# Three RMS norms of a two-block network: per-token roots applied at other places, and the slabs behind them in token halves

## The reference

```python
x = x + mix @ w_out                                   # end of the mixers of block one
h2 = rmsnorm(x, ln2)
x = x + jnp.square(jax.nn.relu(h2 @ w_mlp1)) @ w_mlp2
h3 = rmsnorm(x, ln3)
x = x + jax.nn.sigmoid(h3 @ w_pg) * (p @ w_pp)        # embedding gate
x = rmsnorm(x, ln_f)
# block two, even layer
h = rmsnorm_2(x, pre_g)
u = h @ w_in_ab
qa, ka, va, oa, za, ia, fa, qb, kb, vb, zb = split_cols(u, EVEN_SPLITS)
qk = silu(causal_dwconv(concat([qa, ka]), conv_w))    # 4 taps over the tokens
ig = ia + b_i
lf = log_sigmoid(fa + b_f)
ha = mlstm(q, k, va, ig, lf)
```

## Time and profile before

| | us |
|---|---|
| runs | 2020.83, 2022.13, 2023.01 (median 2022.13) |
| profiled execution | 2020.71 |
| its span | 2019.0 |
| PE busy | 1956.5 (97%) |
| PEld busy | 1617.4 (80%) |
| DVE, ACT, POOL busy | 758.5, 785.1, 844.0 |
| mean granted TensorE clock | 0.992 of full speed |

### The profile page before, as it was taken

How to read it: one execution, slowest core, us unless ns; L and a number is a source line. 1 busy time by engine, 2 the same in 40 slices (tenths; PEclk the granted TensorE clock), 3 DMA queues, 4 the chain that set the end, 5 groups by cost and what they waited for, 6 DMA issues and landing times.

```text
span 2019.0 us, 25217 instructions
## 1 busy us (share of the span) xinstructions
PE 1956.5 (97%) x9056; PEld 1617.4 (80%) x9056; DVE 758.5 (38%) x1184; ACT 785.1 (39%) x1537; POOL 844.0 (42%) x654
## 2 busy tenths in 40 slices
PE   7999999999999999999998999999999999999898
PEld 5777888988887888888886887888787778888787
DVE  4211322440222322222347764312376646015743
ACT  5322443413424433333364443143446535333332
POOL 3523444415354355444342643344333343445452
PEclk9999999999999999999998999999999999999999
DMA  4522333313133223222231422233222231322231
GB/s 140 151 63 71 96 84 84 87 39 110 62 114 111 73 99 110 96 96 94 78 94 42 114 84 63 57 96 91 64 68 74 68 130 62 106 94 89 89 105 52
DMA packets 98583, 176.90 MB, mean 88 GB/s; under 512 B 10747, under 2 KB 16519, under 8 KB 98492
## 3 DMA queue, kind: packets, MB, share of 16 engines
q1 hardware_dynamic: 94212, 170.17, 27.2%
q10 hardware_dynamic: 4280, 5.51, 0.9%
HBM read 171.70 MB, written 3.93 MB: 87 GB/s over the span
## 4 chain that ended last, share of the span: by engine, by line
issue 46%; PE 31%; POOL 20%; DVE 2%; ACT 1%; POOLq 1%; ACTq 0%; DVEq 0%
POOL w_lo L567 20%; PE proj L1735 10%; PE proj L1737 10%; PE proj L1736 10%; DVE arena L1717 1%; ACT arena L814 1%; POOLq L571 0%; DVE act_lo L1148 0%; PE work L1869 0%; DVE arena L1721 0%; POOLq L569 0%; ACT arena L647 0%; DVE arena L1720 0%; PE work L1870 0%; ACT w_hi L843 0%
## 5 line engine op out<-in xcount | busy, mean ns | idle before, releaser
L567 POOL TENSOR_TENSOR w_lo<-w_raw,w_hi 128x512 fp32r<-128x512 f32 x632 | 838.6, 1345 | 1147.0 <-ACT w_hi L592 1007.5
L1735 PE MATMUL proj<-act_hi,w_hi 128*128 128x512 f32 (+1 forms) x1264 | 494.9, 392 | 10.3 <-DVE arena L1450 2.3
L592 ACT CAST w_hi<-w_raw 128x512 fp32r<-128x512 f32 x536 | 313.3, 618 | 479.8 <-PE proj L1737 465.8
L1736 PE MATMUL proj<-act_lo,w_hi 128*128 128x512 f32 (+1 forms) x1264 | 487.3, 385 | 0.0
L1737 PE MATMUL proj<-act_hi,w_lo 128*128 128x512 f32 (+1 forms) x1264 | 486.9, 385 | 0.0
L1735 PE MATMUL proj<-w_hi,act_hi 128*128 128x512 f32 x800 | 321.2, 402 | 9.4 <-DVE arena L1702 4.9
L1737 PE MATMUL proj<-w_hi,act_lo 128*128 128x512 f32 x800 | 312.9, 391 | 0.0
L1736 PE MATMUL proj<-w_lo,act_hi 128*128 128x512 f32 x800 | 312.8, 391 | 0.0
L1735 PEld LDWEIGHTS proj<-act_hi,w_hi 128*128 128x128 f32 x1264 | 238.9, 189 | 62.5 <-POOL w_lo L567 7.3
L1737 PEld LDWEIGHTS proj<-act_hi,w_lo 128*128 128x128 f32 x1264 | 238.8, 189 | 48.1
L1736 PEld LDWEIGHTS proj<-act_lo,w_hi 128*128 128x128 f32 x1264 | 239.0, 189 | 46.1 <-issue 0.5
(11 more groups left out here) (303 smaller groups left out, 1803.5 us busy)
## 6 DMA issues: line engine op xcount, KB each, us to landing
w_raw<-in_w_in SPq DMA_DIRECT2D x154, 256.0 KB, 2.8
w_raw<-in_w_in_ab SPq DMA_DIRECT2D x146, 256.0 KB, 2.6
w_raw<-in_w_mlp SPq DMA_DIRECT2D x128, 256.0 KB, 2.7
w_raw<-in_w_in_c SPq DMA_DIRECT2D x64, 256.0 KB, 2.7
w_raw<-in_w_out_ab SPq DMA_DIRECT2D x32, 256.0 KB, 2.6
w_raw<-in_w_out_c SPq DMA_DIRECT2D x32, 256.0 KB, 2.9
w_raw<-in_w_o_gla SPq DMA_DIRECT2D x16, 256.0 KB, 2.8
w_raw<-in_w_out SPq DMA_DIRECT2D x16, 256.0 KB, 2.6
```

The lines of the kernel that those rows point to most:

```text
L567: return pool.tensor_tensor(w_lo[:, slot, :], w_raw[:, slot, :], w_hi[:, slot, :].bitcast(F32), ALU.subtract)
L592: act.copy(w_hi[:, b % RING, :], w_raw[:, b % RING, :]).then_inc(hi_ready, 1)
L1735: pe.matmul(out_, a_hi, b_hi, start=first, stop=False)
L1736: pe.matmul(out_, a_hi, b_lo, start=False, stop=False)
```

## The change

ln2 (ahead of slab mlp_up 0) and pre0 (ahead of lstm_q 0) are now done token tile by token tile like pre1: mix_out 1 and ple_gate 1 are done by bank, transposes of a finished token tile stand between their matmuls, and mlp_up 0 and lstm_q 0 are done in token halves. The gains ln2 and pre_norm times ln_f are loaded as rows and multiplied in by DVE. For ln3 TensorE transposes the plain x, four tiles inside mlp_down's last slab and four between the two ple_p slabs; the root goes into the scale of the sigmoid. For pre0 the columns carry only the gain; the root even_r is applied when results leave the banks: as a per-partition scale in ACT's copies and gates of v, o, z and sb_v, sb_z, and for q, k, the gate rows, sb_q and sb_k, whose tokens lie along the free axis, as a product on DVE with a row that TensorE spreads from a diagonal matrix. DVE thus takes the 16 bank copies of lstm_q and lstm_k from ACT. lstm_q 0 now stands ahead of lstm_if. ple_sig has four buffers instead of two.

```diff
-    slabs.append(Slab("lstm_if", narrow(w_ab, at_if), 1))
-    for at, name in enumerate(("lstm_q", "lstm_k", "lstm_v")):
+    slab("lstm_q", w_ab, 0)
+    slabs.append(Slab("lstm_if", narrow(w_ab, at_if), 1))
+    slab("lstm_q", w_ab, NCOL)
+    for at, name in enumerate(("lstm_k", "lstm_v")):
...
@@ ScalarE, ln2
-            half_squared(x, 0, (proj_free, mixes[0].bank0))
-            ahead(mixes[1])
-            half_squared(x, 1, (proj_free, mixes[1].bank0)).then_inc(sums_ready, 1)
-            token_root("ln2")
+            halves_squared(x, mixes)
+            s, up0 = mixes[1], by_name["mlp_up"][0]
+            for m in range(MT):
+                own_root(x, s, m)
+                prepare(up0.first + (0, 0, 2, 8)[m])
+                if m:
+                    token_hi("ln2", m - 1, s)
+                prepare(up0.first + (0, 0, 6, 8)[m])
+            token_hi("ln2", MT - 1, s)
...
@@ ScalarE, gate
-                if n >= 2:
-                    act.wait_ge(ple_done, n - 1)
-                act.activation(ple_sig[:, n % 2, :], bank(s, m), ACT.Sigmoid).then_inc(proj_free, 1)
+                if n >= 4:
+                    act.wait_ge(ple_done, n - 3)
+                act.activation(ple_sig[:, n % 4, :], bank(s, m), ACT.Sigmoid, scale=rstd[:, m:m + 1]).then_inc(proj_free, 1)
...
@@ ScalarE, mLSTM
+            prepare(by_name["lstm_q"][1].first + 4)
             act.preload_act_table_set("natural_log_exp_and_others")
             act.wait_ge(lstm_if_copied, 1)
             act.dma_start(row["f"], if_rows[LSTM_HEADS:]).then_inc(lstm_f_moved, 16)
+            prepare(by_name["lstm_q"][1].first + KD)
             act.wait_ge(lstm_f_ready, 1)
...
+            prepare(by_name["lstm_k"][0].first + 3)
             act.wait_ge(lstm_rows, 1)
...
-            for n, s in enumerate(conv_slabs):
+            for n, s in enumerate(conv_slabs[1:]):
+                convolved(n)
                 ahead(s)
-                for c in range(4):
-                    if n:
-                        act.wait_ge(conv_done, 4 * (n - 1) + c + 1)
-                    act.copy(conv_raw[:, c, :], bank(s, c)).then_inc(proj_free, 1)
-                if n:
-                    convolved(n - 1)
...
@@ ScalarE, pre1
-                prepare(z0.first + (0, 0, 1, 5)[m])
+                prepare(z0.first + (0, 0, 2, 7)[m])
...
-                prepare(z0.first + (0, 0, 4, 7)[m])
+                prepare(z0.first + (0, 0, 5, 8)[m])
...
@@ VectorE
+            def embedded(i, m):
+                s, n = by_name["ple_gate"][i], i * MT + m
+                part = slice(i * NCOL, (i + 1) * NCOL)
+                vec.wait_ge(proj_free, s.bank0 + m + 1)
+                g_, xm = ple_sig[:, n % 4, :], x[:, m, part]
+                step(vec.tensor_tensor(g_, g_, ple_pp[:, m, part], ALU.mult))
+                vec.tensor_tensor(xm, xm, g_, ALU.add).then_inc(ple_done, 1)
+                vec.wait_ge(ple_done, n + 1)
+                vec.tensor_tensor(normed_x["pre0"][:, m, part], xm, even_row[:, part], ALU.mult).then_inc(x_normed, 1)
...
+            def raw_rows(n):
+                s = (by_name["lstm_q"] + by_name["lstm_k"])[n]
+                for c in range(4):
+                    if n:
+                        vec.wait_ge(conv_done, 4 * (n - 1) + c + 1)
+                    vec.tensor_tensor(conv_raw[:, c, :], bank(s, c), even_r_row, ALU.mult).then_inc(proj_free, 1)
...
+            raw_rows(0)
+            convolve(0, 0)
+            s = by_name["lstm_if"][0]
+            vec.tensor_tensor(if_rows, bank(s, 0)[0:2 * H, :], even_r_row[0:2 * H, :], ALU.mult).then_inc(proj_free, 1)
...
+            convolve(0, 1)
             vec.wait_ge(lstm_f_moved, 16)
             vec.tensor_scalar(row["f"], row["f"], lstm_b[:, 1:2], None, ALU.add).then_inc(lstm_f_ready, 1)
+            convolve(0, 2)
...
+            convolve(0, 3)
+            raw_rows(1)
...
@@ TensorE
-            slab(by_name["mix_out"][1], "tokens")
+            slab_by_bank(by_name["mix_out"][1], "act", before=early_tiles("ln2", [(2, 1), (3, 1), (3, 7)]))
...
-            slab(ups[0], "features", ready=ready_act("ln2"), before=turn_norm("ln2"))
+            features_by_half(ups[0], "ln2", late_tiles("ln2", [4]))
...
-            slab(by_name["ple_gate"][0], "tokens", ready=ready_act("ln3"), before=turn_norm("ln3"))
-            slab_by_bank(by_name["ple_gate"][1], "act")
...
-            narrow_slab(by_name["lstm_if"][0], 0, ready=ready_act("pre0"), before=turn_norm("pre0", ple_pp))
+            slab(by_name["ple_gate"][0], "tokens", ready=ready_act("ln3"))
+            slab_by_bank(by_name["ple_gate"][1], "act", before=early_tiles("pre0", [(2, 3), (3, 1), (3, 6)]))
...
+                if (half, j) == (0, 3):
+                    turn_tokens("pre0", MT - 1)
+                elif (half, j) == (1, 6):
+                    pe.wait_ge(r_diag_ready, 1)
+                    for m in range(MT):
+                        ins = pe.matmul(work[:, 0, natural(m)], ones, even_diag[:, natural(m)], start=True, stop=True)
+                    ins.then_inc(r_row_full, 1)
+
+            features_by_half(by_name["lstm_q"][0], "pre0", last_tile)
+            narrow_slab(by_name["lstm_if"][0], 0)
+            slab(by_name["lstm_q"][1], "features")
```

More of the change, by code:

```diff
@@ L897, in _ @@
             token_root("ln_f")
-            prepare(second.first + second.n + 5)
-            fill_hi("act", ACT_AT["pre0"], KD, turn=TURN_AT["pre0"], gain=PRE, after=end("ple_gate"))
-            ahead(by_name["lstm_if"][0])
+            prepare(by_name["lstm_q"][1].first + 4)
             act.preload_act_table_set("natural_log_exp_and_others")
@@ L1440, in _ @@
[L1440 to L1442 removed]
                 vec.tensor_scalar(x[:, m, :], ple_pp[:, m, :], rstd[:, m:m + 1], None, ALU.mult).then_inc(x_final, 1)
[L1444 removed]
+            vec.wait_ge(r_row_full, 1)
+            step(vec.tensor_copy(even_r_row, work[:, 0, :]))
             H = LSTM_HEADS
[L1448 removed]
```

392 lines of the change are left out of this document (220 added, 172 removed).

## The result

| | us, median | runs | ratio to before, 95% interval |
|---|---|---|---|
| before | 2022.57 | 4 (2020.83 to 2024.28) | |
| after | 2011.79 | 4 (2009.63 to 2012.25) | 0.9942 [0.9928, 0.9956] |
| after, once more beside the experiments | 2011.07 | 5 (2009.36 to 2011.14) | 0.9946 [0.9933, 0.9960] |

The change gains 10.8 us, 0.5%: faster, as predicted, by less than the 14.9 us of the sum. The profiled execution took 2011.68 us, its span is 2010.0 us, 9.0 less than before.

What follows compares the result with a forecast made beforehand. TensorE, busy for 97% of the span, was taken to bound the kernel. Gains of 2.6 (ln2), 12.0 (ln3 to lstm_q 1) and 0.3 us (pre1), total 14.9, gave 2005.8 us profiled, 2007.2 as median; range 1999 to 2017.

Steps and rivals of the forecast that it cites:

- The exponentials: Ahead of lstm_k, TensorE waits 3.8 us for ACT's four exponentials, part of the stage's 12.0 us gain.
- Rival 1: Exponentials come in time, as DVE's chain is not stretched: 5.8 us more gain, 2001.4 us, chance 0.17.
- The tail of that wait: Behind the wait for the exponentials, a stretch at half clock, costing 2.0 us by ln2's 3.18 us wait.
- The MLP norm: At ln2, from mix_out 1 to mlp_up 0: overhead falls from 9.8 to 7.2 us, gain 2.6 us.
- The relu banks: In mlp_up 1, a wait of about 1.1 us, since mlp_up 0's half slab fills all four banks within 1.4 us.
- lstm_k and behind: DVE gets 16 bank copies, 11.5 us, and late casts just fit in lstm_k 0 and 1: 0 us.
- pre1: Ahead of odd_z 0, earlier casts exchange part of the weights' wait for the bank's: gain 0.3 us.
- No shortage of weights in ple_gate 1: In ple_gate 1, the weights' shortage of 1.9 us goes, with four sigmoid buffers: 0 us left.
- x_normed at pre0: At pre0, the transposes wait 1.2 us for tile 0's second half from DVE, at full clock.
- Bank 0 of lstm_q 1: Ahead of lstm_q 1, TensorE waits 0.9 us to get bank 0 back from the gate rows.
- VectorE busy about 10 us more, ScalarE about 10 less: A sign expected in the profile after: DVE's busy time up about 10 us, ACT's down about 10.
- Rival 2: DVE bounds the mLSTM stage, casts behind silu late in lstm_k 0 and 1: 8 us less gain, 2015, chance 0.13.

Runs made afterwards that it cites:

- rows_split: rows_first, with the rows of lstm_q 1's banks 0 and 1 taken ahead of the last tap of convolve(0, 3); 2011.46 us, ratio 0.9942.
- rows_first: parts_late's edit on the changed kernel, with convolve(0, 2) also moved behind the gate rows; 2009.99 us, ratio 0.9945.
- ln2_undone: The changed kernel with the MLP norm as before the change, everything else as after; 2011.87 us, ratio 0.9961.
- parts_late: The changed kernel with two zero fills moved ahead of lstm_if's rows and neg_e's three steps behind raw_rows(1); 2010.53 us, ratio 0.9948.
- pre1_counts: The changed kernel with only the cast counts in front of odd_z 0 set back to those of before; 2012.44 us, ratio 0.9957.

## Why the prediction was right or wrong

Predicted 2007.2 us (1999 to 2017), measured 2011.8; it was faster by over 0.2%, as said with 0.88. By steps:

- **The exponentials** (the new edge at L2122, now L2226): wait 3.34 us against 3.8, and TensorE started L2226 13.3 us earlier than before, forecast 14.0 (12.0 and the tail of 2.0). The end of VectorE's chain held: L2226 starts 31.9 us behind the end of lstm_q 0, forecast 31.8. Its steps did not, and that the sum came out is in part luck. Convolution 1 was put at 6.1 us beside POOL and took 2.8. ScalarE's casts came only at 1107.1 us, so that POOL's work fell beside convolution 2 (5.6 us) and two operations on 4 partitions (1.5 us each) instead. VectorE was 2.3 us ahead of the forecast at f and 0.6 behind it at the start of L1551. Convolutions 1 and 2 (taps behind the first), VectorE:

```profile
1106.15 2.32 DVE L1529 SCALAR_TENSOR_TENSOR arena<-arena,cols 128x511 f32<-128x511 f32 x3
1110.33 5.07 DVE L1529 SCALAR_TENSOR_TENSOR arena<-arena,cols 128x511 f32<-128x511 f32 x3
```

  Rival 1 did not come.
- **The tail of that wait was mis-sized**: 2.0 us taken from the tail behind ln2's wait, measured 4.2 and 3.2 us in the two traces, 2.0 to 4.2 in seven. The row of ln2 was the wrong one to take: behind L2226 come 20 products of 4 columns first, which are slow at half clock themselves (3.07 against 1.72), and then whole slabs. A nearer row was in the prediction itself, the 3 us that it counts behind the 2.33 us wait of lstm_q 0, where whole slabs follow too. Gain of the stage 9.1 and 10.1 us instead of 12.0: 2.2 and 1.2 are the tail, the rest the later start of L2226. This is the largest error.
- **The MLP norm**: gain 1.6 or 0.4 us, not 2.6. Tile 2's two halves waited 2.2 us and tile 3 not at all, where 1.3 was taken for both tiles; with the products that start late behind them they cost 2.4 (mix_out 1 took 26.9 us to its last product, 21.8 of slab and 2.7 of transposes). The relu banks cost what was forecast: the profile prints 0.4 us of waits in mlp_up 1, counted from the modelled end of a product, but the slab took 23.1 us, 1.2 over 21.8, and the forecast was 1.1. Missed was that tile 2's two products stand beside POOL's w_lo, though the earlier trace rows showed such a stretch for the convolution. And where the clock falls there, 1.3 us more go, which the sum had at nothing.
- **lstm_k and behind, 0 us**: right for weights in the changed kernel (no wait for w_lo in lstm_k), but "it just fits" held in the shelter of the wait and the half clock ahead of it: rows_split, without them, waits 3.4 us for w_lo. Further on 0.6 to 1.7 us were lost between lstm_v and pre1, in all thirteen traces of kernels with the change. About 0.3 lies in lstm_o and lstm_z (a new wait of 0.25 for the scaled silu, L1038), the rest among the sb units, where the waits for the exponential L1062 (L997 before) rose from 3.7 to 4.4 us; no experiment takes it apart.
- **pre1**: 2.1 us instead of 0.3 at full clock; where the clock falls at the same place, 0.2 to 0.6. The step that failed is that the casts would delay the bank by what the weights gain: the bank's wait grew by 0.13 us. This error of 1.8 us the other way hides as much of the others in the total, and that is luck.
- **No shortage of weights in ple_gate 1**: right, and by the cause given, the ring of four. **x_normed at pre0**: 1.4 us against 1.2. **Bank 0 of lstm_q 1**: 0.86 against 0.9. **Root-row products**: 0.81 against 1.0. **Turning for ln3**: 3.33 against 3.5.
- **VectorE busy about 10 us more, ScalarE about 10 less**: only 3 more and 5 less on the page. L1518 does add 10.4 us in 16 operations, but the convolutions fell from 57.1 us in 51 operations to 47.5 us in 61 (1095 to 1190 us of either trace), with POOL idle beside more of them. Why ScalarE fell by 5 only was not followed up.
- **Rival 2** (VectorE bounds the stage, casts behind silus) is not how the changed kernel lost time, and is how every attempt to gain more from the gate rows ended.
- The start (1.6 us more in the trace after than in that of before) and the end stage (0.9 more) hold no changed code. rows_first's and ln2_undone's traces have 28.9 or 29.0 us in the start as before's has, and parts_late's 32.2, so the start is chance. So is the end as far as the traces go: pre1_counts, with the same code there, took 106.2 us, before 106.3 and ln2_undone 107.6, all with the same wait of 4.9 us ahead.

Sum of the stages for after: start -1.6, MLP norm 1.6, mLSTM 9.1, middle -1.3, pre1 2.1, end -0.9: 9.0 us, the difference of the spans. Without start and end, which are chance, the change is worth some 11.5 us in this pair of traces, against the 14.9 forecast.
